# Gated heads of a mixer: query and key weights folded into one matrix, scores and states taken with the features themselves

## What is computed

```python
xc_h, xm_h = features after / before the convolution, per head, [S, 192]
q = einsum('bshd,hde->bhse', xc_h, w_qkv[0])
k = einsum('bshd,hde->bhse', xc_h, w_qkv[1]) * 192 ** -0.5
v = einsum('bshd,hde->bhse', xm_h, w_qkv[2])
# per direction, head and chunk (gates give dexp, iexp, wexp, cexp, floor):
s   = (q @ k.T) * dexp
num = s @ v + iexp * (q @ C);   den = sum(s) + iexp * (q @ n)
h   = num / max(|den|, floor)
C   = cexp * C + sum_s wexp_s k_s v_s^T;   n = cexp * n + sum_s wexp_s k_s
```

## Time and profile before

| | us |
|---|---|
| median of 3 runs | 3321.08 (3320.72 to 3322.37) |
| the profiled execution | 3329.51 |
| its span, first to last instruction | 3327.8 |
| stage with gates and values | from 1186.9 to about 1224 |
| stage with the heads | from 1224.1 to about 1468 |
| first `intra` of heads 0, 1, 2, 3 | 1255.01, 1307.61, 1359.73, 1411.85 |

### The profile page before, as it was taken

How to read it: one execution, slowest core, us unless ns; L and a number is a source line. 1 busy time by engine, 2 the same in 40 slices (tenths; PEclk the granted TensorE clock), 3 DMA queues, 4 the chain that set the end, 5 groups by cost and what they waited for, 6 DMA issues and landing times. The chain is left out here.

```text
span 3327.8 us, 52854 instructions
## 1 busy us (share of the span) xinstructions
PE 3120.3 (94%) x20701; PEld 2514.0 (76%) x20701; DVE 1877.8 (56%) x3566; ACT 1319.4 (40%) x2403; POOL 394.5 (12%) x321
## 2 busy tenths in 40 slices
PE   7999997999999989969799999799989989999999
PEld 6896675888867767867588888488856678896567
DVE  5535747658657725685656556724366543435654
ACT  2006823647642134551356555511345420134442
POOL 0100201334330000020133324100000000000000
PEclk9999998999999989989799999999999999999999
DMA  7525425779866300012568667610000220100022
GB/s 224 156 75 166 142 92 202 304 282 372 333 260 179 115 22 1 16 49 108 209 250 326 277 242 295 235 34 27 26 17 1 108 103 21 39 26 17 1 84 82
DMA packets 204509, 459.29 MB, mean 138 GB/s; under 512 B 56355, under 2 KB 131447, under 8 KB 195577
## 3 DMA queue, kind: packets, MB, share of 16 engines
q1 hardware_dynamic: 185849, 389.04, 32.6%
q0 software_dynamic: 18432, 67.12, 5.3%
HBM read 381.17 MB, written 72.22 MB: 136 GB/s over the span
## 5 line engine op out<-in xcount | busy, mean ns | idle before, releaser
L1863 PE MATMUL psum<-high_in,e_rowsT_high 128*128 128x256 f32 (+1 forms) x1080 | 330.6, 324 | 5.4 <-DVE e_rowsT_low L175 5.4
L1864 PE MATMUL psum<-high_in,e_rowsT_low 128*128 128x256 f32 (+1 forms) x1080 | 326.7, 321 | 0.0
L175 POOL TENSOR_TENSOR low_down<-w_down,high_out 128x1024 fp32r<-128x1024 f32 x64 | 205.0, 3221 | 299.8 <-ACT high_out L1941 299.8
L1863 PEld LDWEIGHTS psum<-high_in,e_rowsT_high 128*128 128x128 f32 x1080 | 206.8, 192 | 22.4 <-issue 6.2
L1864 PEld LDWEIGHTS psum<-high_in,e_rowsT_low 128*128 128x128 f32 x1080 | 207.3, 192 | 16.3
L175 DVE TENSOR_TENSOR low_gate<-w_gate,high_in 128x1024 fp32r<-128x1024 f32 x128 | 148.0, 1219 | 7.7 <-ACT high_in L1941 7.0
L175 DVE TENSOR_TENSOR low_up<-w_up,high_in 128x1024 fp32r<-128x1024 f32 x128 | 148.0, 1221 | 0.0
L3795 DVE CUSTOM_DVE_ANT_0 mla_probs<-psum,mla_mask 128x512 f32<-128x512 f32 (+2 forms) x192 | 96.8, 554 | 74.1 <-PE psum L3666 62.8
L1868 PE MATMUL psum<-low_up,e_rowsT_high 128*128 128x256 f32 x720 | 130.5, 283 | 0.0
L1941 ACT ACTIVATE high_out<-w_down 128x1024 fp32r<-128x1024 f32 x128 | 124.7, 1050 | 9.1 <-DMA w_down<-in_exp_w_down 9.0
L1941 ACT ACTIVATE high_in<-w_gate 128x1024 fp32r<-128x1024 f32 x128 | 124.8, 1058 | 6.7 <-issue 6.7
(11 more groups left out here) (612 smaller groups left out, 7477.2 us busy)
## 6 DMA issues: line engine op xcount, KB each, us to landing
w_gate<-in_exp_w_gate SPq DMA_DIRECT2D x32, 2048.0 KB, 8.4
w_up<-in_exp_w_up SPq DMA_DIRECT2D x32, 2048.0 KB, 13.4
w_down<-in_exp_w_down SPq DMA_DIRECT2D x32, 2048.0 KB, 20.1
ada<-in_ada_w SPq DMA_DIRECT2D x24, 1024.0 KB, 7.4
expert_rows<-e_out POOLq DMA_DIRECT2D x47, 512.0 KB, 7.1
expert_rows<-zero_row SPq DMA_DIRECT2D x33, 512.0 KB, 6.9
token_rows<-x SPq DMA_DIRECT2D x32, 512.0 KB, 2.6
x<-token_rows SPq DMA_DIRECT2D x24, 512.0 KB, 7.0
```

The costliest lines, as they stand in the source:

```text
L175: return eng.tensor_tensor(low, whole, high, ALU.subtract)
L1863: pe.matmul(dst, rows_high[:, k, :], w_high[:, k, cols], start=(k == 0), stop=False)
L1864: pe.matmul(dst, rows_low[:, k, :], w_high[:, k, cols], start=False, stop=False)
```

## The change

q k^T is xc (Wq Wk^T) xc^T. So Wq and Wk are turned by TensorE (`turned_w`, 8 pieces of four transposes) and multiplied once for each head into one matrix of 256 by 256 (`fold`, 4 pieces of four matmuls with 256 columns, scaled by 192^-0.5). The items `qk` become one projection of the features with it, in two tiles of 128 instead of two of 96, with no k beside q: 4 items a head. The items `keys` are gone. The scores are the projected features times `xcT` itself, the states are sums over the features by token instead of over the keys; these rows (`xrows`) come from 16 pieces of three transposes of `xcT`. The pieces are made in `gates_and_values`, in TensorE's order before and between the value pieces; ScalarE empties their banks. State, update and q now have 128 partitions instead of 96, and the weighted rows 256 columns instead of 192. Buffers move. Waits on the `keys` semaphores become waits on `raw` or `qk`.

```diff
@@ gates_and_values
+    turned_w = [m.at("ml_wqkT", AT_X + at * KB, [HF, ML_HEADS, 2, 2 * P]) for at in (0, 8)]
+    W3 = ML_W // 2
...
-    pieces = [(h, t) for h in range(ML_HEADS) for t in range(TILES)]
+    values = [("value", h, t) for h in range(ML_HEADS) for t in range(TILES)]
+    turned = [("turned_w", h, a) for h in range(ML_HEADS) for a in range(2)]
+    folds = [("fold", h, 0) for h in range(ML_HEADS)]
+    rows = [("rows", t, part) for t in range(TILES) for part in range(2)]
+    pieces = rows + values[0:6]
+    first_turned = len(pieces)
+    for n, w in enumerate(turned):
+        pieces += [w, values[6 + n]]
+    neg_at = len(pieces)
+    for n, w in enumerate(folds):
+        pieces += [w] + values[14 + 4 * n:18 + 4 * n]
+    pieces += values[30:]
...
+                    if kind == "rows":
+                        for k in range(3):
+                            mm = pe.transpose(dst[:, k * P:(k + 1) * P], xcT[:, 3 * t + k, h * P:(h + 1) * P], c["ident"])
+                    if kind == "turned_w":
+                        for k in range(4):
+                            half, j = divmod(k, 2)
+                            mm = pe.transpose(dst[0:HF, k * P:(k + 1) * P], wq.of(t, h, j)[:, half * HF:(half + 1) * HF], c["ident"])
+                    if kind == "fold":
+                        if h == 0:
+                            pe.wait_ge(s["values_copied"], neg_at)
+                        for j in range(2):
+                            for half in range(2):
+                                mm = pe.matmul(dst[:, j * 2 * P:(j + 1) * 2 * P], turned_w[0][:, h, half, j * P:(j + 1) * P], turned_w[1][:, h, half, :],
+                                               start=(half == 0), stop=(half == 1))
...
             mm.then_inc(s["gates_turned"], 1)
+            produce(0, 10)
             pe.wait_ge(s["summands_ready"], 1)
             pe.matmul(bank[0][:, 0:H], c["upto"], lf[:, 0:H], start=True, stop=True)
...
+            produce(10, len(rows))
+            pe.wait_ge(s["a_ready"], 1)
+            pe.transpose(bank[1][0:S, 0:P], a[:, :], c["ident"]).then_inc(s["a_turned"], 1)
             pe.wait_ge(s["weights_loaded"], 16 * wq.loads)
             pe.wait_ge(s["weights_cleared"], 6)
-            values(0, 3)
...
-            values(3, 6)
+            produce(len(rows), first_turned)
...
-            values(6, 20)
+            produce(first_turned, neg_at)
...
-            values(20, len(pieces))
+            produce(neg_at, len(pieces))
@@ HeadItems
-        self.per_head = {"qk": 8, "keys": 4, "spread": 4, "raw": 2}
-        self.steps = [[qk[0], spread[0]], [qk[1]], [qk[2], spread[1]], [qk[3]], [qk[4], spread[2]], [qk[5]], [qk[6], spread[3]], [qk[7]],
-                      [keys[0]], [raw[0]], [raw[1]], [keys[1]], [keys[2]], [keys[3]], [], []]
+        self.per_head = {"qk": 4, "spread": 4, "raw": 2}
+        self.steps = [[spread[0]], [qk[0]], [spread[1]], [qk[1]], [spread[2]], [qk[2]], [spread[3]], [qk[3]],
+                      [], [raw[0]], [raw[1]], [], [], [], [], []]
@@ heads
-            sp.wait_ge(s["keys_ready"], 4 * ML_HEADS)
+            sp.wait_ge(s["qk_ready"], 4 * ML_HEADS)
...
                     for j, f in pieces_of(H):
-                        mm = pe.matmul(dst[0:HF, :], wq.of(a, H, j)[:, n * HF:(n + 1) * HF], xcT[:, f, cols], start=(j == 0), stop=(j == 1))
+                        mm = pe.matmul(dst, fold[:, H, j, n * P:(n + 1) * P], xcT[:, f, cols], start=(j == 0), stop=(j == 1))
...
-                        for k in range(2):
-                            mm = pe.matmul(dst[:, (chunk % 4) * P:(chunk % 4 + 1) * P], kT[:, k, q], qT[H % 2][:, k, q], start=(k == 0), stop=(k == 1))
+                        for k, f in pieces_of(H):
+                            mm = pe.matmul(dst[:, (chunk % 4) * P:(chunk % 4 + 1) * P], xcT[:, f, q], qT[H % 2][:, k, q], start=(k == 0), stop=(k == 1))
...
-                            mm = pe.matmul(bank[6 + u % 2][0:HF, k * 256:k * 256 + DV], kw[:, at % 3, k * HF:(k + 1) * HF], vals[:, chunk, h, :],
+                            mm = pe.matmul(bank[6 + u % 2][:, k * 256:k * 256 + DV], kw[:, at % 3, columns_in_pair(h, f)], vals[:, chunk, h, :],
...
-                        act.activation(kw[:, at % 3, :], keys[h % 2][:, chunk, :], ACT.Copy,
+                        act.activation(kw[:, at % 3, :], xrows[chunk][:, pair_of_tiles(h)], ACT.Copy,
```

More of the change, by code:

```diff
@@ L2131, in ml_layer @@
     hs = m.at("ml_hs", AT_X, [P, TILES, ML_HEADS, ML_DH])
-    table = gates_and_values(nc, core, gatesT, wq, xmT, vals)
-    heads(nc, core, xcT, wq, vals, table, hs)
+    last = TILES - 1
+    xrows_first = m.at("ml_xrows", W + 96 * KB, [P, last, ML_W])
+    xrows = [xrows_first[:, t, :] for t in range(last)] + [m.at("ml_xrows", W + 61 * KB, [P, ML_W])[:, :]]
+    fold = m.at("ml_fold", W, [P, ML_HEADS, 2, 2 * P])
+    table = gates_and_values(nc, core, gatesT, wq, xmT, vals, xcT, xrows, fold)
+    heads(nc, core, xcT, xrows, fold, vals, table, hs)
     memT = m.at("ml_memT", W + 40 * KB, [P, 2, SEQ])
@@ L2234, in __init__, with gates_and_values @@
         self.a, self.E, self.nuT = a, E, nuT
-def gates_and_values(nc, core, gatesT, wq, xmT, vals):
+def gates_and_values(nc, core, gatesT, wq, xmT, vals, xcT, xrows, fold):
     m = core.mem
@@ L2325, in _ @@
             act.activation(ab[:, :], ab[:, :], ACT.Ln, bias=c["ones"][:, 0:1]).then_inc(s["log_ready"], 1)
-            for n, (h, t) in enumerate(pieces):
+            for n, (kind, h, t) in enumerate(pieces):
+                src = bank[5 + n % v_banks]
                 act.wait_ge(s["values_ready"], n + 1)
-                act.activation(vals[:, t, h, 0:ML_DH], bank[5 + n % v_banks][:, 0:ML_DH], ACT.Copy).then_inc(s["values_copied"], 1)
+                if kind == "value":
+                    act.activation(vals[:, t, h, 0:ML_DH], src[:, 0:ML_DH], ACT.Copy).then_inc(s["values_copied"], 1)
+                if kind == "rows":
+                    act.activation(xrows[h][:, t * W3:(t + 1) * W3], src[:, 0:W3], ACT.Copy).then_inc(s["values_copied"], 1)
+                if kind == "turned_w":
+                    act.activation(turned_w[t][:, h, :, :].rearrange("p n d -> p (n d)"), src[0:HF, :], ACT.Copy).then_inc(s["values_copied"], 1)
+                if kind == "fold":
+                    act.activation(fold[:, h, :, :].rearrange("p j d -> p (j d)"), src, ACT.Copy, scale=ML_DH ** -0.5).then_inc(s["values_copied"], 1)
             act.wait_ge(s["exponents_ready"], 1)
@@ L2398, in __init__ @@
     def __init__(self):
-        self.per_head = {"qk": 8, "keys": 4, "spread": 4, "raw": 2}
-        qk, keys, spread, raw = [[(kind, i) for i in range(n)] for kind, n in self.per_head.items()]
-        self.steps = [[qk[0], spread[0]], [qk[1]], [qk[2], spread[1]], [qk[3]], [qk[4], spread[2]], [qk[5]], [qk[6], spread[3]], [qk[7]],
-                      [keys[0]], [raw[0]], [raw[1]], [keys[1]], [keys[2]], [keys[3]], [], []]
+        self.per_head = {"qk": 4, "spread": 4, "raw": 2}
+        qk, spread, raw = [[(kind, i) for i in range(n)] for kind, n in self.per_head.items()]
+        self.steps = [[spread[0]], [qk[0]], [spread[1]], [qk[1]], [spread[2]], [qk[2]], [spread[3]], [qk[3]],
+                      [], [raw[0]], [raw[1]], [], [], [], [], []]
         self.order = [item for step in self.steps for item in step]
@@ L2420, in two_earlier, with heads @@
         return kind0, self.count(kind0, H0, i0)
-def heads(nc, core, xcT, wq, vals, table, hs):
+def heads(nc, core, xcT, xrows, fold, vals, table, hs):
     m = core.mem
@@ L2432, in heads @@
     DV = ML_DH + 2
[L2433 to L2436, removed]
+    qT = [m.at("ml_qT", W + at * KB, [P, 2, SEQ]) for at in (32, 40)]
+    decay = [m.at("r_decay", W + at * KB, [P, DIRS, TILES, P]) for at in (18, 48)]
     raw = m.at("r_raw", W + 26 * KB, [P, TILES, P])
[L2438 to L2442, removed]
+    state = m.at("r_state", AT_XT + 24832, [P, DIRS, 2, 2, DV])
+    kw = m.at("r_kw", W + 56 * KB, [P, 3, 2 * P])
+    carried = m.at("r_carried", W + 59 * KB, [P, 2, DV])
+    num = m.at("r_num", AT_XT + 31040, [P, 2, DV])
+    den = m.at("r_den", W + 60 * KB + 576, [P, U])
     stats = m.at("hn_stats", W + 30 * KB, [P, ML_HEADS, TILES, 6])
@@ L2470, in item_bank, with qk_of, columns_in_pair, pair_of_tiles @@
         return bank[4 + items.at(kind, i) % 2]
-    def qk_of(H, j):
-        a, n, half = j // 4, j // 2 % 2, j % 2
-        return a, n, slice(half * BANK, (half + 1) * BANK), (kT if a else qT[H % 2])
+    def qk_of(j):
+        n, half = divmod(j, 2)
+        return n, slice(half * BANK, (half + 1) * BANK)
+    def columns_in_pair(h, f):
+        first = min(tile for _, tile in pieces_of(h))
+        return slice((f - first) * P, (f - first + 1) * P)
+    def pair_of_tiles(h):
+        first = min(tile for _, tile in pieces_of(h))
+        return slice(first * P, (first + 2) * P)
     def features(t, f):
@@ L2480, in last_head_of @@
         return ((f + 1) * P - 1) // ML_DH
```

(8 more changed lines are left out.)

39 lines of the change are left out of this document (16 added, 23 removed).

## The result

The changed kernel takes 3306.37 us (median of 5 runs, 3302.42 to 3307.13), the kernel before, measured beside it, 3322.37 (3320.72 to 3324.19). The medians differ by 16.0 us; the ratio with its 95% interval is 0.9947 [0.9933, 0.9960], which is 17.6 us of 3322. A second measurement gave 0.9948 [0.9934, 0.9962]. The forecast was 24.5 us less. So the median lies above the 3290 to 3303 of the forecast, inside the whole range (3285 to 3311), and nearest to the 3308 of rival (A); the traces have to tell the two apart. The profiled execution took 3302.42 us, the fastest of the five.

A forecast was written before the change was run, and what follows sets the result against it. TensorE was taken to bound the head loops, with VectorE late in each head's second half after the change. -28.5 - 9.4 + 13.4 = -24.5 us, from the median 3321.1 to 3296.6; forecast 3290 to 3303, whole range 3285 to 3311.

The forecast's parts named there:

- rival (A): Head loops: unit chain is the bound, 0.60 us waits before the sum stay, 46 us a head, 3308; chance 0.19.
- Head loops, -28.5: Heads 0 to 2: without half the `qk` and all `keys` items, 128.3 us instead of 156.8.
- The update's 128 weight columns: Head loops: loading 128 columns instead of 96 taken as 0, at most 1.5 us a head.
- the state on 128 partitions: VectorE in the head loops: same 0.61 us as on 96; 2.8 us a head if it grew with partitions.
- (B): Rival, head loops: VectorE is no hindrance, 39.7 us a head, 3285; chance 0.12.
- Preparation of head 0, -9.4: Stage before the head loops: 21.4 us instead of 30.8, ending with the chain raw, copy, multiplication.
- Gates and values, +13.4: Stage before head 0's preparation: added rows, turned weights and folds move its end from 1221.1 to 1234.5.
- A fold: TensorE, gates and values: four 256-column matmuls, 1.7 us by columns, range 1.3 to 3.6.
- six value pieces: Gates and values, kernel before: 6 pieces run at half clock, read from 4.17 us for the first 12 records.
- Head 3, 0: Last head: prepares nothing, begins with VectorE about 3.7 us behind as before, and runs as before.
- Rival (C), the clock: Head loops: TensorE, no longer dense, granted 1.2 GHz; 110 us lost, 3406; chance 0.04.
- The rule named with (C): Head loops: small pauses between matmul groups, from cycling through PSUM banks, can make the clock swing between two levels.

The follow-up runs named there:

- alone: Kernel before plus rows, turned weights and folds in the gates and values stage, unused by its unchanged heads: ratio 1.0038.
- second pair: Second traces of the kernel before and the changed kernel, both unchanged; measured again at ratios 1.0003 and 0.9948.

## Why the prediction came out as it did

**Head loops, -28.5: right, as was its reason.** From unit 8 of head 1 (1321.84) the `intra` of units 9 to 12 start at 1.64, 5.07, 8.50 and 10.15 (forecast 1.65, 5.1, 8.5, 10.2), unit 15's at 16.50 (16.4) and the next head's at 18.09 (18.0). Units 0 to 7 take 24.97 us (24.0 and 0.9). VectorE's waits before the sum, which rival (A) kept everywhere, fell from 7.0 us a head (12 of them) to 4.3 (8). This, and not the total, rules (A) out. The update's 128 weight columns cost nothing that shows; the state on 128 partitions takes 0.61 us, as on 96. So (A) and (B) are out: a head takes 42.0 to 43.1 us at the full clock (up to 45.2 in the second trace, with falls), not 46 or 39.7. The sum of three heads, -28.5, holds in the first trace; in the second it is -24.5, with a fall behind each wait.

**Preparation of head 0, -9.4: right.** Measured -10.7 and -7.7. What moves it is the granted clock behind the 3.10 us change of stage: in the kernel before 6.8 us at 1.2 GHz go with 30.9 us and 3.4 with 29.2, in the kernel after 3.4 with 20.2 and 6.8 with 21.5.

**Gates and values, +13.4: right, a little high.** +11.9 and +12.7, alone +12.0. A fold costs 1.73 (1.72 taken), and the sums are late by the rows pieces before them. The values began 1.5 us earlier than forecast, mostly since the last six rows pieces and the sums took less (2.95 us, 4.0 in the forecast). The forecast also read six value pieces of the kernel before as made at half the clock; the 4.17 us are 12 records, which is three pieces. The sum didn't use the six.

**Head 3, 0: off by 1.7 us in the first pair, by 0.1 in the second.** In the first trace after it begins with 6.8 us at the lower clock.

**Rival (C), the clock: dismissed by one trace.** The step that failed is "Against: in head 3, with TensorE busy only 11.6 of 16 us, the clock stays at 1.00", and with it the price of nothing for the clock. It was true of the one trace that the forecast had. The second trace of the unchanged kernel shows the same stretch of head 3 with a fall, right behind the wait of 2.71 us that is in both:

```profile
1428.90:1444.90 16.00, 12.99 (x68) 11.72 (x68) 14.89 (x47) 7.82 (x15) 0.00 (x0) 0.89 0.01 2
```

```profile
1438.88 1.00 PE L2549 MATMUL psum<-ml_v,r_decay 128*128 128x194 f32 x2 [2.71 <-DVE r_num L2744]
```

Twelve of the fourteen traces have this wait in head 3, and in ten of the twelve the clock falls at its end or right behind it; the trace before the change is one of the two without. So a second trace of the kernel before would have spoken for (C) and not against it. (C) came in part: no head ran at 1.2 GHz throughout, but starts of heads did, for 3 to 7 us each, at a different head from trace to trace. With useless matmuls in the waits the ratio goes from 0.9948 to 0.9929 and 0.9922, and 0.0078 of 3322 us is 26 us, near the 24.5 forecast without (C). The intervals touch, and the traces account for 0.3 to 5.6 us in heads 0 to 2, so the size of this gain is less sure than its direction. That such a wait brings the fall is shown by the count: 20 of 26 unfilled, none of eight filled. What decides whether a given wait does stays open: the same wait in the same kernel did in one trace and not in the other, and a wait of 1.13 us was followed by a fall in one kernel and by none in another.

The rule named with (C), from the Trainium skill ("TensorE: Matmul & The Clock Gate", section "A second HAM failure mode: psum-queue depth-cycling"), was nearer than the forecast made it. The wait before unit 15 is one for a PSUM bank, which the sum of unit 13 must free, and the traces after agree that the clock swings behind it (0.64 over 4.7 us). The price was less than a tenth of that of (C): 6 to 9 us by the ratios, of 110. Two ways to end the wait itself were not tried: a third bank for `intra` (all eight are in use), and another order on VectorE, with the sum that TensorE waits for ahead of the multiplication.

**The rest of the program.** It differs by 7 us between two traces of the same kernel before (3046.6 and 3039.8 us), more than what the second pair above misses. So the spans of two traces can't tell what became of the 5 us; the stages can, and the ratios.

## What to carry to other kernels

Walk through the units of a loop with its own waits before trusting the larger of two engines' sums: here that gave 42.9 us where the sums said 39.7, and 43.1 was measured. When work is taken from TensorE, price the wait that appears twice, once for itself and once for the clock after it; filling it, with the next head's work or with work that nobody reads, is a cheap trial. Don't dismiss a fall of the clock by one trace: here the second trace of the same kernel said the opposite. Work moved off a late engine must not land in a queue ahead of what that engine waits for (ScalarE here), or beside it on GpSimd.

## What was not expected of the hardware

- With eight useless matmuls of 128 columns in each wait of 1.9 us before unit 15, the ratio went from 0.9948 [0.9934, 0.9962] to 0.9929 [0.9917, 0.9941], about 6 us.
- The same stretch of the same kernel (head 3, behind a wait of 2.71 us) had PEclk 1.00 in one trace and 0.89 in the next.
- In each of three heads a VectorE instruction took 2.3 instead of 0.42 us beside a GpSimd multiplication of 128x1024 elements (two in 4.79 us).
- A table load on ScalarE (1.28 us) cost nothing while ScalarE had to wait, and stood in the chain once copies were put ahead of it.
